# Two row loads of a bidirectional scan go from SyncE's queue to GpSimd's

## The reference

```
def step(S, inp):                                   # DeltaNet, one chunk
    u_i, w_i, kt_i, gl_i = inp[:4]
    v_new = u_i - einsum("bhld,bhdv->bhlv", w_i, S)
    if with_output:
        qg_i, qk_i = inp[4:]
        o = einsum("bhld,bhdv->bhlv", qg_i, S) + einsum("bhij,bhjv->bhiv", qk_i, v_new)
    S = S * exp(gl_i)[..., None, None] + einsum("bhld,bhlv->bhdv", kt_i, v_new)
...
def step(h, inp):                                   # state space, one chunk
    B_i, C_i, xdt_i, a_i = inp
    y_off = einsum("bgin,bghnp->bghip", C_i, h) * exp(a_i)[..., None]
    h = h * exp(a_last)[..., None] + einsum("bgjn,bghjp->bghnp", B_i, xdt_i * exp(a_last - a_i)[..., None])
...
decay = where(tri, exp(where(tri, Acs[..., :, None] - Acs[..., None, :], 0.0)), 0.0)
scores = einsum("cbgin,cbgjn->cbgij", Cc, Bc)[:, :, :, None] * decay
y_diag = einsum("cbghij,cbghjp->cbghip", scores, xdt)
```

## Time and profile before

| | us |
|---|---|
| median of 3 runs | 1323.39 |
| lowest and highest run | 1323.25, 1328.37 |
| the profiled execution | 1324.75 |
| its span, first to last instruction | 1323.0 |

### The profile page before, as it was taken

How to read it: one execution, slowest core, us unless ns; L and a number is a source line. 1 busy time by engine, 2 the same in 40 slices (tenths; PEclk the granted TensorE clock), 3 DMA queues, 4 the chain that set the end, 5 groups by cost and what they waited for, 6 DMA issues and landing times.

```text
span 1323.0 us, 15648 instructions
## 1 busy us (share of the span) xinstructions
PE 1206.3 (91%) x6022; PEld 683.3 (52%) x6022; DVE 753.2 (57%) x1075; ACT 418.8 (32%) x1062; POOL 229.1 (17%) x203
## 2 busy tenths in 40 slices
PE   4999999999998999979888999991799999999992
PEld 3555545555544554568777744451444444444440
DVE  5298999887935788559888656658300101010116
ACT  5334233213111111667767544431010101010113
POOL 0300000010000011158686200001100101010112
PEclk9999999999998999989999999996899999999996
DMA  9923355442133443367878755526699999999967
GB/s 365 297 80 95 113 181 155 139 154 96 48 117 90 90 97 93 88 193 232 240 227 256 269 205 191 191 80 242 229 334 352 320 352 318 354 316 352 320 220 195
DMA packets 200407, 274.02 MB, mean 207 GB/s; under 512 B 65365, under 2 KB 114510, under 8 KB 200334
## 3 DMA queue, kind: packets, MB, share of 16 engines
q1 hardware_dynamic: 180422, 215.82, 49.8%
q0 software_dynamic: 13840, 50.86, 12.5%
q10 hardware_dynamic: 6072, 6.35, 1.4%
HBM read 221.03 MB, written 51.97 MB: 206 GB/s over the span
## 4 chain that ended last, share of the span: by engine, by line
PE 71%; DVE 14%; DMA 5%; issue 4%; ACT 3%; SPq 2%; POOLq 0%; DVEq 0%; ACTq 0%
PE ps L2143 23%; PE ps L1298 17%; PE ps L1321 8%; PE ps L1251 7%; PE ps L475 2%; DVE arena L2583 2%; DVE arena L2512 2%; DVE arena L2581 2%; DMA arena<-w_in 1%; DMA arena<-ada_w 1%; PE ps L2042 1%; DMA scan_dram<-arena 1%; DVE arena L725 1%; PE ps L1287 1%; PE ps L569 1%
## 5 line engine op out<-in xcount | busy, mean ns | idle before, releaser
L2143 PE MATMUL ps<-arena 128*128 128x512 f32 (+1 forms) x1072 | 425.3, 554 | 4.6 <-DMA arena<-w_in 4.6
L2143 PEld LDWEIGHTS ps<-arena 128*128 128x128 f32 x1072 | 201.8, 191 | 205.5 <-issue 195.6
L1298 PE MATMUL ps<-arena 128*128 128x512 f32 x512 | 225.2, 593 | 1.5 <-DVE arena L1652 0.8
L2512 DVE SCALAR_TENSOR_TENSOR arena<-arena,taps 128x1024 f32<-128x1024 f32 x160 | 207.3, 1296 | 5.5
L1298 PEld LDWEIGHTS ps<-arena 128*128 128x128 f32 x512 | 95.9, 190 | 115.8 <-issue 113.8
L1658 DVE TENSOR_TENSOR arena<-arena,ps 128x512 f32<-128x512 f32 x16 | 11.0, 688 | 215.6 <-PE ps L1298 215.6
L1251 PE MATMUL ps<-arena 128*128 128x512 f32 x256 | 115.5, 597 | 1.3 <-DMA arena<-w_out 0.9
L1321 PE MATMUL ps<-arena 128*128 128x512 f32 x256 | 112.5, 592 | 0.0
L1321 PEld LDWEIGHTS ps<-arena 128*128 128x128 f32 x256 | 47.5, 190 | 54.0 <-issue 54.0
L1251 PEld LDWEIGHTS ps<-arena 128*128 128x128 f32 x256 | 46.5, 190 | 51.8 <-issue 49.5
L1469 ACT ACTIVATE arena<-ps 128x512 f32<-128x512 f32 x16 | 9.6, 598 | 197.6 <-PE ps L1298 197.6
(11 more groups left out here) (352 smaller groups left out, 1552.7 us busy)
## 6 DMA issues: line engine op xcount, KB each, us to landing
arena<-exp_w_gate SPq DMA_DIRECT2D x16, 2048.0 KB, 11.4
arena<-exp_w_up SPq DMA_DIRECT2D x16, 2048.0 KB, 9.4
arena<-exp_w_down SPq DMA_DIRECT2D x16, 2048.0 KB, 10.1
arena<-ada_w POOLq DMA_DIRECT2D x16, 1024.0 KB, 6.6
arena<-w_in SPq DMA_DIRECT2D x28, 512.0 KB, 3.9
arena<-ada_w SPq DMA_DIRECT2D x4, 2048.0 KB, 19.6
arena<-x SPq DMA_DIRECT2D x16, 512.0 KB, 7.3
arena<-g_dram SPq DMA_DIRECT2D x16, 512.0 KB, 5.0
```

The source lines that it names most:

```text
L1298: last = mm(ps[gu_bank[s] + j][:], xsT[s][:, k, :], ew[s][j][:, k, :], start=(k == 0), stop=(k == KD - 1))
L2143: last = mm(ps[3 * (m % 2) + gi][:, 0:w], wring[(m + 1) % NW][:, k, :], hT[:, k, o:o + w], start=(k == 0), stop=(k == KD - 1))
L2512: ins = v.scalar_tensor_tensor(accg, cin_l[ci % 2][:, j // 3:j // 3 + GR, j % 3:j % 3 + GW], tp[:, j:j + 1], accg, ALU.mult, ALU.add)
```

## The change

`load_qk` and `load_e8` are no longer issued by SyncE but by GpSimd, at the end of its turn for a step, with the same waits. The order of the two is turned: qk comes first. GpSimd's loop issues them from s = 0 on whenever `two` is a latent step. In SyncE's loop nothing takes their place.

```diff
@@ pool_scan
+            def load_qk(step):
+                d, n = step
+                if nl(step) > 0:
+                    pool.wait_ge(sem("s_op"), turn(d, nl(step)))
+                pool.dma_start(flat(QE[d]), qk_dram[tile_of(step)]).then_inc(sem(f"ld_qk{d}"), 16)
+
+            def load_e8(step):
+                d, n = step
+                if nl(step) > 0:
+                    pool.wait_ge(sem("s_fc"), turn(d, nl(step)))
+                r = (tile_of(step) * 2 + d) * GD + DN_H
+                pool.dma_start(flat(E8[d]), g_dram[r:r + SSM_H].rearrange("g p -> (g p)").unsqueeze(0)
+                               .to_broadcast([P, SSM_H * P])).then_inc(sem(f"ld_e8{d}"), 16)
+
...
                 if lat(nxt):
                     query_e(nxt)
+                if s >= 0 and lat(two):
+                    load_qk(two)
+                    load_e8(two)
@@ sp_scan
-            def load_e8(step):
-                d, n = step
-                if nl(step) > 0:
-                    sp_.wait_ge(sem("s_fc"), turn(d, nl(step)))
-                r = (tile_of(step) * 2 + d) * GD + DN_H
-                sp_.dma_start(flat(E8[d]), g_dram[r:r + SSM_H].rearrange("g p -> (g p)").unsqueeze(0)
-                              .to_broadcast([P, SSM_H * P])).then_inc(sem(f"ld_e8{d}"), 16)
-
-            def load_qk(step):
-                d, n = step
-                if nl(step) > 0:
-                    sp_.wait_ge(sem("s_op"), turn(d, nl(step)))
-                sp_.dma_start(flat(QE[d]), qk_dram[tile_of(step)]).then_inc(sem(f"ld_qk{d}"), 16)
...
                 if four and s % 2 == 1:
                     load_at(three)
                     load_at(four)
-                if lat(two):
-                    load_e8(two)
-                    load_qk(two)
                 if two and two[1] < LAST:
                     load_kt(two)
```

## The result

The time went up. Median after 1330.67 us (1327.20 to 1338.82, 20 runs), before 1324.01 us (1318.48 to 1333.19, 20 runs) in the same sessions: ratio 1.0048, 95% interval [1.0032, 1.0064]. The profiled run took 1329.57 us for a span of 1327.8 us, 4.8 us more than before. In a second comparison the same kernel stood at 1.0084 [1.0055, 1.0114]. The forecast was 1319.4 us, 4.6 us under this median of before; the time came out 6.7 us over it, outside the range of 1313.0 to 1327.5.

The account below looks back on a forecast made before the run. Waits, not a full engine, bound it: VectorE in half one, the diagonal-block transfer in half two. 3.6 us (blocks) plus 1.2 (two pairs) less 0.8 (late e8) gave 4.0 us sooner: 1319.4 us, range 1313.0 to 1327.5.

Parts of the forecast that it names:

- qk goes into the gap: Scan: qk issued by GpSimd about 648.8 us while DMA idles, taking 1.0 to 1.1 us of transfer from the burst.
- the issues taken off SyncE: SyncE's queue: without e8 and qk, everything behind goes 0.84 us sooner; together with qk's move, blocks land 0.9 us sooner.
- hidden anyway: Rival: full DMA engines pass the same bytes in another order; 0 to 1.2 us gained, about 1323; chance 0.20.
- The sum: Scan pairs: 4 x 0.9 = 3.6 us plus 1.2, less 0.8 for late e8; net 4.0 us sooner.
- The masks, −1.0 us: Half one, VectorE L725: with L838 pushed past 650.3, the third mask ends 1.0 us sooner.
- Half one's gain: Odd step's solve to even's: shorter masks cut TensorE's wait for rest, 3.8 us at most over six pairs.
- the two pairs without that wait: Pairs where no block transfer ends half two: half one's gain stays, 0.57 + 0.66 = 1.2 us.
- e8 late: VectorE's masks: e8 issued by GpSimd lands just in time; 0.8 us taken off for a few late ones.
- third rival: Slower: late e8 delays masks and solve, 7x - 4.8 us, turning at x = 0.7; up to 1329; chance 0.18.
- half two: Even step's solve to odd step's solve: said to hang on the diagonal-block transfer; four pairs' waits together 8.0 us.
- GpSimd's issues: GpSimd: 32 more issues at 0.543 us, 17 us in all, with 49 us free; cost taken as nothing.
- The cover for L838: GpSimd, half two: L838 waited 1.82 us for its own row anyway, so two issues are covered.

Follow-up runs that it names:

- e5: The changed kernel with one GpSimd wait holding the first pair of moved loads until the step before has passed to_s; ratio to before 1.0028.
- e11: The same kernel as e5, run again; ratio to before 1.0020.
- e10: Second profile of the unchanged kernel before; no ratio; third block_near 31.5 us behind the first, with 1.43 us idle.
- e6: Kernel before with only the 16 qk loads moved to GpSimd, the first held until the step before passed to_s; ratio to before 1.0011.
- e7: Kernel before without the qk loads behind each direction's first latent one (2 of 16 left, values left out); ratio to before 0.9968.
- e1: Changed kernel with the first loads (steps 4 and 5) kept on SyncE, the other 28 on GpSimd; ratio to before 1.0010.
- the four early ones: Profiles with the first pair ahead of kg and the blocks: the changed kernel, its repeat, e2 and e3; ratios to before 1.0039 to 1.0084.
- e2: Kernel before with only the loads of steps 4 and 5 moved to GpSimd, at the changed kernel's place; ratio to before 1.0042.
- e3: Kernel before, all loads on SyncE, but step 4's qk and e8 issued ahead of its kg rows and diagonal blocks; ratio to before 1.0039.
- e8: Kernel before plus two small GpSimd transfers (one 512-byte row each) behind each query_e of a latent step; ratio to before 1.0060.
- e9: e7 plus the small GpSimd transfers of e8; ratio to before 1.0116, 1339.84 us.
- e12: Kernel before plus only GpSimd's wait for from_chunk behind each latent query_e but a direction's first, no load moved; ratio to before 1.0003.
- e4: Kernel before plus two small GpSimd transfers (128 rows of 4 bytes each) behind each latent query_e; ratio to before 1.0731, 1420.31 us.

## Why the prediction was wrong

**The change part by part: "qk goes into the gap" and the issues taken off SyncE, 4 x 0.9 = 3.6 us.** Void. The block loads did not land 0.9 us sooner but 0.6 us later at the median of all 80 (5.1 against 4.5; with the first pair held 4.4 and 4.8, in e5 and e11), and e8 took 6.2 instead of 5.0. In the six pairs the idle time ahead of L462 is 1.25 to 2.65 us, where it was 0 to 2.36, and 0.99 to 1.92 in e10. This is the rival "hidden anyway": the same bytes pass, in another order. Its ground, a DMA share of 1.22, was in the same rows as the gap that I trusted, and e6 and e7 together show that in the steady pairs the bytes and not their order set the landing. The Trainium skill, DMA: Bandwidth & Descriptors, section "Issuing engines are not separate DMA queues", says that issuing from more engines saves the time to issue alone; e1 agrees, with nothing gained from 28 loads.

**The step that failed and made it slower: a price per pair, with no look at the pair that has no wait.** The loads of steps 4 and 5 carry no wait for a reader before them. The sum priced what the loads pass on SyncE's queue in the steady pairs and multiplied by the pairs; it has no term for the first one. On its new engine the first pair passed kg and the even blocks. It costs some 3.6 us at that place (the mean of the four early ones' thirds, 33.9, less the 30.4 of the eleven others; with the late third of e6 among the others 3.2), and 0.4% of the time, some 5.4 us, in e2 and e3. The half clock behind the wait may be the difference: 6.0 us of it in the mean of the four early profiles against 2.3 in the twelve others are at most 1.8 us, an estimate from the clock rows that no run tests. Rows of before for this were there to be read: SyncE's issues from 572.94 (L903) to 577 us, and GpSimd's L848, the last work ahead of the new issues, ending at 572.75.

**The masks, −1.0 us.** The size was right: three masks take 3.73 to 4.45 us in the six half ones instead of 4.73 to 5.45, the third one 0.68 us in five of the six, and waits for L750 went from 6.7 to 1.7 us. The reason was half wrong. I let L838 come later because GpSimd is busy issuing, and took the issues as harmless to VectorE. With a product ready behind them they are not: e8 and e9 show 0.6 us more a mask. What helped was GpSimd's wait for `from_chunk`, so that the size came out is in part luck. I had written that wait down, for e8's due time, and not as the thing that lets the mask in.

**Half one's gain ends in the wait for the blocks.** Right, and e12 is its clean case: 5.8 us of waits for L750 gone, 5.8 us more ahead of L462 (4.2 and 3.7 against e10). The 1.2 us for the two pairs without that wait did not show in any ratio, and half of it had no ground: the pair with the 0.57 us is followed by a `block_near` at 619.48 that waited 0.75 us in the same trace. The last pair, with the 0.66 us, has no such wait there or in e10.

**e8 late.** Taken at 0.8 us; the waits for it grew from 0.7 us in two masks to 6.5 in seven, since it landed 1.2 us later than the 5.0 that I used. This is the third rival's mechanism: 0.27 to 1.53 us each, 0.9 in the mean, where that rival's sum turns at 0.7. But in the six steady pairs it fell into half two, which waits for the blocks anyway, and TensorE's waits for L750 were 1.7 us in all; so not much of it can have come through `rest`. How much of it reached the end can't be told from the 0.1 to 0.3% that remain in e1, e5 and e11.

**GpSimd's issues.** 0.56 us each against 0.543 taken: right. The cover for L838 held: no wait of TensorE in the scan is ended by GpSimd.

## What to carry to other kernels

When a load moves to another engine's queue, walk through its first instances by themselves: those without a wait go as soon as the new engine gets there, and can land in front of transfers that the old queue's order had protected; one wait of the right kind puts them back. When the DMA engines work off a burst behind the wait that you want shorter, count bytes, not order. A VectorE operation that takes turns with GpSimd's products gets its turn while GpSimd waits, and not beside an issue with a product ready behind it, so a wait can be worth more than a filler. And profile the kernel before twice: what two profiles of it don't agree on is no sign in a third.

## What the runs showed of the hardware

- **A GpSimd issue with a product ready behind it gives a VectorE addition with two SBUF inputs no turn.** An addition that began beside such an issue took 2.36 to 2.45 us in 15 of 15 cases (e8, e9, e4), until 0.56 us past the product's end. Where no product was ready it took 0.69 us beside an issue of 0.56 us (one case, e4), and 0.68 with GpSimd waiting (e12). One that was already running when an issue began (0.36 us in, after) took 0.68. The Trainium skill, SBUF — State Buffer, section "Who interferes with whom", infers that such an addition and the making of descriptors need different ports. The 0.69 us agrees; what keeps the addition in the 15 cases, before the product's own row begins, no run here shows.
- **Small rows in the way are dear.** 32 transfers of 128 rows of 4 bytes cost 96 us, 3.0 us each. The blocks of step 4, issued at 578.73, were in after 17.7 us instead of 4.0:

```profile
577.07 1.16 POOL L895 DMA_DIRECT2D idle_dram<-eps  x2
578.73 1.80 SPq L932 DMA_DIRECT2D arena<-xy_dram  x4
596.43 0.65 PE L464 MATMUL ps<-arena 32*32 32x32 f32 x32 [14.12 <-DMA arena<-xy_dram]
```

  The same 32 as one row of 512 bytes each left the block landings at 4.3 us (median) and cost 8 us, of which the longer masks are a part. The Trainium skill, DMA: Bandwidth & Descriptors, section "Specifications", says that transfers under 512 bytes are done by reading and writing back; the rows agree that they are dear, and only the runs give the price.
- **Loads moved to a second queue land at each other's cost.** With qk and e8 on GpSimd, qk landed in 4.0 instead of 5.7 us, e8 in 6.2 instead of 5.0 and the blocks in 5.1 instead of 4.5 (medians; in e5, with the first pair held, 4.5, 5.7 and 4.4). How much of it is the queue and how much the new place in time, no run separates.
- **SyncE's issues slow down under load:** four small ones took 1.80 us before, 3.28 us behind two large loads that GpSimd had just begun, and 3.12 us in e3, where SyncE had issued the two large ones itself.
